# Gates finished in the projection, retention in another order, one weight piece a tile

## The reference

```python
fq, fk, fv, fl, rq, rk, rv, g = split(rms_norm(h) @ w_in)      # rotary on rq, rk
fo = fox_attention(fq, fk, fv, logf)                           # softmax attention with forget gates
ro, S = retention(rq, rk, rv)                                  # chunks of 128, state S carried over
ro = (ro - mean(ro)) / sqrt(var(ro) + eps) * gn_w              # per head of 64
mix = concat(fo, ro) * silu(g) @ w_out
h = h + mix
h = h + sigmoid(h @ ple_gate_w) * rms_norm(p @ ple_proj) * ple_norm_w
```

## Time and profile before

| What | us |
|---|---|
| median of 3 runs (lowest, highest) | 4097.49 (4090.81, 4100.02) |
| the profiled execution, its own time | 4094.79 |
| its span in the trace | 4093.0 |
| projection half 1, about | 438 to 838 |
| retention, about | 2307 to 2536 |
| tail 0, about | 2537 to 3043 |

### The profile page before, as it was taken

One profiled execution on the slowest core, in us unless ns is written; L12 is line 12 of the kernel. 1 busy time (PEld: TensorE's weight loads), 2 busy tenths in 40 slices (PEclk: granted clock), 3 DMA queues, 4 the chain that ended last, 5 costly groups with the idle time before them and its releaser, 6 DMA issues. The chain is left out here.

```text
span 4093.0 us, 65190 instructions
## 1 busy us (share of the span) xinstructions
PE 3539.3 (86%) x21092; PEld 2654.0 (65%) x21092; DVE 1653.5 (40%) x3100; ACT 1379.3 (34%) x2379; POOL 415.3 (10%) x663
## 2 busy tenths in 40 slices
PE   6999799955799899899999675999968949959998
PEld 5888688833455555565565464788856737748887
DVE  3222311133345444444454265433335646643333
ACT  3111200012233333333333364333335656643223
POOL 0000000001022122122222242000000000000000
PEclk9999899957799999999999887999989979979999
DMA  5233522255577777777776565433334243252221
GB/s 151 104 130 122 160 99 99 91 115 167 158 234 233 219 234 216 221 225 232 233 234 185 160 217 210 143 128 124 119 130 149 83 142 108 72 171 87 87 82 58
DMA packets 375887, 627.51 MB, mean 153 GB/s; under 512 B 125177, under 2 KB 175137, under 8 KB 375586
## 3 DMA queue, kind: packets, MB, share of 16 engines
q1 hardware_dynamic: 333810, 487.62, 36.8%
q0 software_dynamic: 41792, 136.48, 10.5%
HBM read 488.74 MB, written 135.22 MB: 152 GB/s over the span
## 5 line engine op out<-in xcount | busy, mean ns | idle before, releaser
L1549 PEld LDWEIGHTS att_samp_ps_t<-att_ident,att_samp_k_ring 128*128 128x128 f32 x2048 | 237.8, 146 | 282.0 <-issue 231.7
L1549 PE MATMUL att_samp_ps_t<-att_ident,att_samp_k_ring 128*128 128x128 f32 x2048 | 338.6, 290 | 85.5 <-DVE att_samp_kt L1354 44.4
L123 PE MATMUL in_ps_z<-in_w_hi,in_u_hi 128*128 128x512 f32 x952 | 374.1, 393 | 38.6 <-DVE in_w_lo L156 38.6
L1149 POOL DMA_DIRECT2D att_samp_v_ring<-cache_v x512 | 274.8, 537 | 985.0 <-issue 983.2
L124 PE MATMUL in_ps_z<-in_w_lo,in_u_hi 128*128 128x512 f32 x952 | 373.0, 392 | 0.0
L125 PE MATMUL in_ps_z<-in_w_hi,in_u_lo 128*128 128x512 f32 x952 | 372.8, 392 | 0.0
L1239 ACT COPY att_samp_kt<-att_samp_ps_t 128x512 f32<-128x512 f32 x256 | 149.8, 585 | 502.3 <-PE att_samp_ps_t L1549 501.1
L1354 DVE COPY att_samp_kt<-att_samp_ps_t 128x512 f32<-128x512 f32 x256 | 176.1, 688 | 292.4 <-PE att_samp_ps_t L1549 287.5
L1503 PE MATMUL att_fox_ps_o<-att_fox_prob,att_fox_v_one 128*65 128x512 f32 (+3 forms) x640 | 286.9, 532 | 3.8 <-ACT att_fox_prob L1208 3.8
L1303 DVE TENSOR_REDUCE att_fox_part_max<-att_fox_ps_n 128x1 f32<-128x512 f32 (+2 forms) x320 | 195.0, 609 | 128.8 <-PE att_fox_ps_n L1470 112.9
L1208 ACT ACTIVATE att_fox_prob<-att_fox_ps_k 128x512 f32<-128x512 f32 (+1 forms) x320 | 169.9, 536 | 189.3 <-DVE att_fox_ps_k L1322 112.2
(11 more groups left out here) (364 smaller groups left out, 6765.0 us busy)
## 6 DMA issues: line engine op xcount, KB each, us to landing
att_samp_v_ring<-cache_v POOLq DMA_DIRECT2D x512, 256.0 KB, 3.8
att_samp_k_ring<-cache_k SPq DMA_DIRECT2D x512, 256.0 KB, 3.5
tail_a_hi<-a_hi SPq DMA_DIRECT2D x34, 512.0 KB, 5.8
tail_a_lo<-a_lo SPq DMA_DIRECT2D x34, 512.0 KB, 6.1
in_w_stage<-w_in_even SPq DMA_DIRECT2D x64, 256.0 KB, 6.4
lru_u_hi<-u_hi SPq DMA_DIRECT2D x8, 2048.0 KB, 8.0
lru_u_lo<-u_lo SPq DMA_DIRECT2D x8, 2048.0 KB, 13.1
in_x<-x SPq DMA_DIRECT2D x17, 512.0 KB, 3.8
```

Source lines behind the costliest of these rows:

```text
L123: pe.matmul(out, act_hi, w_hi, start=start, stop=False)
L1149: pool.dma_start(v_ring[:, p, g, :], row(io["cache_v"], page)).then_inc(vp_in[y], 16)
L1549: last = pe.transpose(ps_t[:, a * PAGE:(a + 1) * PAGE], k_ring[:, n % 2, p, a * P:(a + 1) * P], ident[:, :])
```

## The change

Three things. In `in_proj` 1 the gates are finished: ACT makes half the gate and the tanh of half of it, DVE makes SiLU, POOL multiplies the second half with the norm weight (which is now fetched here), and what is stored is SiLU.

In `retention` tanh, SiLU and the norm weighting are gone. q, k, v have four buffers, decayed q three, scores and both output halves two. Turned q and k run one tile further ahead, scores too; the cut of tile t-1 now lies in DVE's step t behind the gated rows, and the state addition ahead of the reciprocal.

The projection and output weights of `tail` 0 (20 pieces) lie in memory from before the retention on (`TailWeights`), with two stage buffers. Tile 0 of the retention takes four pieces, each later tile one: SP loads it, ACT casts it, POOL subtracts. `tail` 0 then loads only the gate weights, through the four buffers in u's space. `tail` 1 stays as it was.

```diff
 in_proj, half 1:
-        by_act = [0, 1] if first else [1, 2]
+        by_act = [0, 1] if first else [1, 2, 3]
+        gated = [] if first else [2, 3]
 SP:     if not first:
+                sp.dma_start(gn[:, :], io["ret_gn_w"][0:1, :].broadcast_to([P, W])).then_inc(consts_in, 16)
 ACT:
+                    if g in gated:
+                        act.wait_ge(*silu_made.at(t - 1, g - 2))
+                        act.activation(half_z[:, g - 2, :], ps_z[:, g, :], ACT.Copy, scale=0.5)
+                        act.activation(tanh_z[:, g - 2, :], ps_z[:, g, :], ACT.Tanh, scale=0.5).then_inc(evac[g].sem, 1)
 POOL:
+                    pool.wait_ge(*silu_made.at(t, 1))
+                    pool.tensor_tensor(z[:, 3, :], silu_z[:, :], gn[:, :], ALU.mult).then_inc(gate_weighed.sem, 1)
 DVE:
+                        dve.scalar_tensor_tensor(out=z[:, g, :] if g == 2 else silu_z[:, :], in0=tanh_z[:, g - 2, :], scalar=1.0,
+                                                 in1=half_z[:, g - 2, :], op0=ALU.add, op1=ALU.mult).then_inc(silu_made.sem, 1)
...
 retention(nc, io, held):
+        def two(t):
+            n = len(held.pieces)
+            return (min(t + 3, n) if t else 0), min(t + 4, n)
 SP:
             for t in range(T):
-                if prompt(t + 3):
+                held.load(sp, *two(t))
+                if prompt(t + 4):
                     sp.wait_ge(*u_done.at(t))
-                    fetch_qkv(t + 3)
+                    fetch_qkv(t + 4)
...
                 sp.wait_ge(*a_low.at(t))
+                sp.dma_start(row(io["a_hi"], t), a_hi[:, t % 2, :].bitcast(F32)).then_inc(a_stored[t % 2], 16)
+                sp.dma_start(row(io["a_lo"], t), a_lo[:, t % 2, :].bitcast(F32)).then_inc(a_stored[t % 2], 16)
 POOL:
+            decay_k(0)
+            gate_fox(0)
             for t in range(-1, LAST):
                 if prompt(t + 1):
-                    decay_k(t + 1)
                     scale_state(t + 1)
-                weigh_gates(t + 1)
+                if prompt(t + 2):
+                    decay_k(t + 2)
+                if t + 2 <= LAST:
+                    gate_fox(t + 2)
+                held.make_low(pool, *two(t + 1))
 ACT, step(t):
                 act.activation(var[:, 2, :], var[:, 1, :], ACT.Sqrt).then_inc(rooted.sem, 1)
-                if prompt(t + 2):
-                    place(t + 2)
-                if t < LAST:
-                    tanh_gate(t + 1)
+                if prompt(t + 3):
+                    place(t + 3)
+                held.make_high(act, *two(t))
                 if prompt(t + 1):
                     keep_o(t + 1)
 DVE, step(t), behind the reduction and var_made:
+                if prompt(t):
+                    add_update(t)
                 dve.wait_ge(*rooted.at(t))
...                                               # reciprocal, normalized rows, gated rows
+                if t:
+                    cut(t - 1)
                 if prompt(t + 2):
                     decay_scores(t + 2)
+                if prompt(t + 3):
+                    decay_q(t + 3)
 PE:
             for t in range(T):
                 if prompt(t + 2):
-                    turn_qk(t + 2)
+                    score(t + 2)
                 if prompt(t + 1):
                     attend(t + 1)
                 turn_gated(t)
                 if prompt(t + 1):
                     turn_rows(t + 1)
                     add_to_state(t + 1)
-                if prompt(t + 2):
-                    score(t + 2)
+                if prompt(t + 4):
+                    turn_qk(t + 4)
...
 trunk:
-        retention(nc, io)
-        tail(nc, io, 0)
+        with ExitStack() as kept:
+            held = TailWeights(Phase(nc, kept, "held"), io, 0)
+            weights = SplitWeights(held.ph, held.pieces, 2)
+            retention(nc, io, weights)
+            tail(nc, io, 0, held, weights)
 tail, where the weights are kept:
+            gate_weights = SplitWeights(ph, more, 0, us)      # us: the four halves of u_hi and u_lo
```

More of the change, by code:

```diff
@@ L225, in in_proj, with kept @@
         products = ph.count("products")
+        silu_made = ph.count("silu_made", 2)
+        gate_weighed = ph.count("gate_weighed")
+        def kept(g, t):
+            return silu_made.at(t, 0) if not first and g == 2 else gate_weighed.at(t) if not first and g == 3 else evac[g].at(t)
         block = ctx.enter_context(nc.Block())
@@ L1627, in _, with retention @@
             each_tile(pe, step, H, peel=2)
-def retention(nc, io):
+def retention(nc, io, held):
     with ExitStack() as ctx:
@@ L1678, in retention @@
         gate_in = [ph.sem(f"gate_in{x}") for x in range(2)]
-        a_stored = ph.sem("a_stored")
+        a_stored = [ph.sem(f"a_stored{x}") for x in range(2)]
         state_stored = ph.sem("state_stored")
@@ L1883, in add_update, with cut @@
                 last.then_inc(added.sem, 1)
[L1885 to L1891, removed]
+            def cut(t):
+                dve.wait_ge(*a_high.at(t))
+                dve.tensor_tensor(a_lo[:, t % 2, :], ps_a[:, :], a_hi[:, t % 2, :].bitcast(F32), ALU.subtract).then_inc(a_low.sem, 1)
             def step(t):
@@ L1958, in attend @@
                 for a in range(PAIRS):
-                    pe.matmul(ps_o[:, a, :], state[:, a].rearrange("p n e -> p (n e)"), q_dec[:, t % 2, a, :], start=a == 0, stop=False,
+                    pe.matmul(ps_o[:, a, :], state[:, a].rearrange("p n e -> p (n e)"), q_dec[:, t % DB, a, :], start=a == 0, stop=False,
                               skip_group_check=True)
@@ L2006, in _, with __init__, by_piece, tail @@
                     add_to_state(t + 1)
-                if prompt(t + 2):
-                    score(t + 2)
-def tail(nc, io, layer):
+                if prompt(t + 4):
+                    turn_qk(t + 4)
+class TailWeights:
+    def __init__(self, ph, io, layer):
+        self.ph = ph
+        pk = PLE // P
+        self.wp_hi = ph.sb("wp_hi", [P, pk, D], F32R)
+        self.wp_lo = ph.sb("wp_lo", [P, pk, D], F32R)
+        self.wo_hi = ph.sb("wo_hi", [P, KC, D], F32R)
+        self.wo_lo = ph.sb("wo_lo", [P, KC, D], F32R)
+        out = (io["w_out_odd"] if layer else io["w_out_even"])[0]
+        self.pieces = by_piece(io["ple_proj"][layer], self.wp_hi, self.wp_lo, pk) + by_piece(out, self.wo_hi, self.wo_lo, KC)
+def by_piece(src, hi, lo, kc):
+    cols = [slice(g * G, (g + 1) * G) for g in range(2)]
+    return [(src[k * P:(k + 1) * P, c], hi[:, k, c], lo[:, k, c]) for c in cols for k in range(kc)]
+def tail(nc, io, layer, held=None, weights=None):
     with ExitStack() as ctx:
@@ L2017, in tail @@
         PK = PLE // P
[L2018 to L2019 removed]
+        kept = held is not None
+        if not kept:
+            held = TailWeights(ph, io, layer)
+        wo_hi, wo_lo, wp_hi, wp_lo = held.wo_hi, held.wo_lo, held.wp_hi, held.wp_lo
         wg_hi = ph.sb("wg_hi", [P, KC, D], F32R)
         wg_lo = ph.sb("wg_lo", [P, KC, D], F32R)
[L2022 to L2031 removed]
+        more = by_piece(io["ple_gate_w"][layer], wg_hi, wg_lo, KC)
         PROJ, OUT, GATE = 2 * PK, 2 * PK + 2 * KC, 2 * PK + 4 * KC
@@ L2047, in tail @@
         u_lo = ph.sb("u_lo", [P, D], F32R) if first else None
-        weights = SplitWeights(ph, pieces, 2 if first else 6,
-                               [u[:, g * G:(g + 1) * G].bitcast(F32) for u in (u_hi, u_lo) for g in range(2)] if first else ())
+        if kept:
+            us = [u[:, g * G:(g + 1) * G].bitcast(F32) for u in (u_hi, u_lo) for g in range(2)]
+            ahead = len(held.pieces)
+            gate_weights = SplitWeights(ph, more, 0, us)
+        else:
+            ahead = 0
+            weights = SplitWeights(ph, held.pieces + more, 6)
+            gate_weights = weights
+        gate_base = GATE - len(gate_weights.pieces)
         stat = ph.sb("stat", [P, 8])
@@ L2117, in _ @@
             fetch_p(1, 1)
-            weights.load(sp, 0, PROJ)
+            if not kept:
+                weights.load(sp, 0, PROJ)
             fetch(0, 0)
-            weights.load(sp, PROJ, OUT)
+            if not kept:
+                weights.load(sp, PROJ, OUT)
             fetch(1, 1)
-            weights.load(sp, OUT, GATE)
+            gate_weights.load(sp, OUT - gate_base, GATE - gate_base)
             def step(t, i, par):
@@ L2318, in gate @@
                 for g in range(2):
-                    pe.wait_ge(weights.low, OUT + (g + 1) * KC)
+                    pe.wait_ge(gate_weights.low, OUT + (g + 1) * KC - gate_base)
                     pe.wait_ge(*mixed.at(t - 1, g))
```

174 lines of the change are left out of this document (86 added, 88 removed).

## The result

The changed kernel takes 4130.14 us (median of 4 runs, 4127.06 to 4132.39); the kernel before took 4094.15 beside it (4 runs, 4090.24 to 4100.02). The ratio is 1.0086, 95% interval [1.0069, 1.0104]: 36 us slower, where 4118 had been forecast. The span of the profiled execution went from 4093.0 to 4125.4 us.

A forecast was written before the change was run, and what follows sets the result against it. TensorE bounds the second projection half, a chain the retention. Retention 33.8, first tail -15.5, projection end 2.6, norm weight 0.6, kept weights' phase 0.7 sum to +22.2 us: forecast 4118 us (chance 0.64), range 4088 to 4140.

The forecast's parts named there:

- The loop: Retention, from one cut's end to the next: a chain through the piece's landing and ACT's cast, 13.5 us against 12.06.
- the landing: Retention: a piece issued third, behind the tile's two stores, lands 4.3 us after its issue.
- the gated rows: DVE's step in the retention tile between normalized rows and cut, taken at 0.69 us.
- rival C: Retention: POOL's fox gating and DVE's gated rows hold each other, up to 1.05 us a tile, time 4133; chance 0.11.
- the centring: TensorE's eight matmuls in each retention tile, behind ACT's copy of o: 1.94 us after idling, 1.06 at the high clock.
- The opening: Start of the retention: four pieces through two buffers in tile 0 move the first cut's end from 2348.5 to 2355.9.
- The last two steps: End of the retention: no copy of o, but a piece is cast; 11.45 and 8.05 us, together 19.5.
- The first tail: Head of `tail` 0: two weight families already there, gate starts 16.7 us sooner, gain taken as 15.5 (12 to 18).
- the kept weights' phase: The kept weights close a phase of their own, costing 0 to 3.2 us, taken as 0.7.
- The projection: Second projection half: gates hidden by TensorE's matmuls, uncovered end +2.6 us, norm weight's fetch +0.6.
- A: Retention: the piece does not wait for the stores and lands in 2.4 us; loop 11.6, time 4088; chance 0.12.
- B: Retention: the landing is not on the path, TensorE sets the loop, some 8.5 us, time about 4035; chance 0.13.

The follow-up runs named there:

- one part alone: The changed kernel with the three `held` calls taken out of the retention, so finished gates and new order without weight pieces: 4069.13 us, 0.9924 of the kernel before.

## Why the prediction was right, and where its sizes were off

**The mechanism** held: a transfer issued only in the step that needs it, and a cast that stands ahead of the tile's own work. The wait stands where it was put, on ACT for a piece, and taking away the late issue takes the loss of the piece away, and what then still stood in the loop was the late fetch of q, k and v.

**The loop** was forecast at 13.5 and is 15.08; over 14 loops that is 22 of the 24 us by which the retention was mis-sized. The term that failed most is the landing. I took 4.3, the median of `rq` in that place; the median is 5.0, and of the tile above the cast starts 5.73 after the cut where 5.20 was summed. The second is the gated rows: 0.69 was taken, and they took 1.23 in the mean of the 14 loops, as POOL's gating (2462.80, 1.29) lies over them. That is rival C's mechanism. I had given it as an alternative to the forecast, and it came on top of it: 0.5 a tile. In the last two tiles, where nothing of POOL's lies beside them, they take 0.69 again. The Trainium skill ("SBUF — State Buffer", who interferes with whom) says that a DVE instruction with two SBUF inputs contends with a POOL one that reads SBUF; 1.27 against 0.69 agrees. The third is small: the centring ended by 2.11 after it began, at 1.2 GHz (granted clock 0.50 from 2457.8 to 2460.0) after 5.31 us of idle, where 1.94 was taken. The rest of the tile, some 0.2 in all, is hops below 0.1 that the sum left out, where the engines hand over.

**The opening** came out to the tenth, 7.4 us longer, but by two errors that cancel: o of tile 1 was copied 0.8 sooner than forecast, and the cut came 8.8 instead of 7.7 behind it, from the same loop terms. The last two steps took 20.96 where 19.5 were summed.

**The first tail** gained 13.9, where the forecast with the kept weights' phase was 14.8. The gate starts 16.4 sooner, counted from the first turn of p (forecast 16.7). By the terms given, the 60 matmuls sum to 15.9 and not to the 15.6 written; they took 16.3. The second half of the gate weights, split through four buffers, then stopped TensorE for 2.6 us, where 1.2 was taken.

**The projection** lost 4.05: 2.5 at its uncovered end (forecast 2.6), 0.2 ahead of its first matmul, where 0.6 was taken for the norm weight's fetch, and 1.4 between its first matmul and its last group, where nothing was taken. The gates of the tiles are not that 1.4: it is complete at the 96th matmul, 34.4 us after the first (33.0 before), and it is 1.4 at the 400th as well. Most of it is a stretch just behind TensorE's last wait for a split weight: eight matmuls from 481.32 to 484.29 took 0.60 to 0.63 us at the low clock (granted 0.50 from 481.3 to 484.6), where those of the kernel before took 0.39 to 0.40 (granted 1.00 from 482.2 to 485.5); why the clock fell there is open. So the gates of all tiles but the last are hidden.

**What brought the total near the forecast** is luck. The terms that belong to the change sum to +47.5, not +22.2; the total moved by 32 in the profiles and by 36 in the medians, since the code from the forget gates to attention, the same in both, was 13.8 us shorter in the profile of after. Without that the total would have been about 4142, just outside the forecast's range of 4088 to 4140. Attention alone, from its first fetch to the retention, took 1379.4 before and 1361.0 to 1375.3 in the eight profiles of after and of the experiments, all with the same code there. Eight profiles scatter by 14 us; whether the 1379.4 lies above them by more than chance cannot be told from one profile. The medians moved by 36 too and not by 47.5, so unless the changed stages themselves vary from run to run, some 11 us of it is in every run; what would make the same code shorter there is open.

**The rivals.** *A*, that the piece would not be held up by the stores, was wrong: 2.9 us in front of them, 4.8 to 5.0 behind. *B* was wrong for this kernel, and its price stood on a missing step: with the landing hidden the next late thing is the fetch of q, k and v, which gave 4063 and not 4035. With that fetch moved too, the loop is 8.40 where B had summed 8.5, and the time 4033. So B's sum of the engines' work came out, though the bytes' 8.2 lie as near; the list of transfers issued behind the cut was incomplete.

**What stays open.** How far the late landing behind the stores, and its scatter (loops of 13.4 to 16.3), come from the order in SP's queue or from the bytes in flight was not separated.

## What to carry to other kernels

Where work is made to ride along in a loop, follow each of its instructions on its in-order queue, and ask what was issued when: a transfer issued behind the last instruction of a step and needed in the next one makes a loop of its own, whatever the busy shares say. Here the cure was an earlier issue; two buffers for the pieces and four for q, k and v had not hidden the wait. When a wait of this kind is taken away, list all other transfers issued at that same point, since the next of them may be late at once, as q, k and v were here. And try the parts alone: here one part alone was worth 29 us and the other cost some 60, and with the fetches issued sooner the two together were worth 66.

## What was not expected of the hardware

A variance step on 128x8 elements, which takes 0.17 us in all tiles but one of the changed kernel, took 0.92 to 0.95 where it fell beside POOL's two-input operations (DVE and POOL of the kernel with the earlier load):

```profile
2402.20 1.27 POOL L1810 TENSOR_TENSOR ret_k_decayed<-ret_qkv,ret_k_table 128x512 f32<-128x512 f32 x1 [0.29 <-PE ret_ps_u L2002]
2402.55 0.95 DVE L1929 TENSOR_SCALAR ret_var<-ret_var 128x8 f32<-128x8 f32 x1
```

It ends at 2403.50, when POOL's operation ends (2403.47): the small operation seems to wait for the large one's end. The kernel with q, k and v sooner tells this from a shared rate, since there POOL's operation has run for different times when DVE's begins (its POOL and DVE timelines):

```profile
2434.25 1.29 POOL L1819 TENSOR_TENSOR ret_state<-ret_state,ret_state_table 128x512 f32<-128x512 f32 x1
2435.30 0.26 DVE L1931 TENSOR_SCALAR ret_var<-ret_var 128x8 f32<-128x8 f32 x1
...
2458.84 1.26 POOL L1819 TENSOR_TENSOR ret_state<-ret_state,ret_state_table 128x512 f32<-128x512 f32 x1
2458.88 1.25 DVE L1931 TENSOR_SCALAR ret_var<-ret_var 128x8 f32<-128x8 f32 x1
```

Begun 1.05 us behind POOL's it takes 0.26, begun 0.04 behind it 1.25, and both end 0.02 to 0.03 after POOL's. The order counts too: in the kernel with the cast last, the gated rows take 1.80 us where POOL's gating began 0.04 before them, 1.11 to 1.15 where it began 0.69 to 0.70 before, and 0.69 where it began 0.04 after. So the one that begins second waits for the first here, as with a lock; no run changed this alone.

In the kernel with q, k and v sooner, where the transfers are at 0.94 of the time, issuing the two `g` transfers of a tile took SP 1.06 to 2.24 us in the loops, against 0.84 to 0.92 in the loops of the changed kernel. The place of that issue among the others differs as well, so that the cause is not shown.
